# Local and selected attention of a head as one stream with one exponential over two score banks

## The reference, cut to what matters

```python
o_cmp, p_cmp = compressed_attention(q, k_cmp, v_cmp, slopes)      # 127 compressed keys
sel_idx = select_blocks(p_cmp, T)                                 # top 16 of 32 blocks of 64 keys
o_slc = selected_attention(q, k_slc, v_slc, sel_idx, slopes)      # softmax over the selected blocks
o_win = window_attention(q, k_win, v_win, slopes)                 # softmax over the last 512 keys
gates = sigmoid(g + gate_b)
o_nsa = gates[..., 0:1] * o_cmp + gates[..., 1:2] * o_slc + gates[..., 2:3] * o_win
```

## Time and profile before

| | |
|---|---|
| median of 3 runs | 1835.87 us (1835.27 to 1837.19) |
| the profiled execution's own time | 1841.42 us |
| its span, slowest core | 1840.4 us (cores 1823.4 to 1840.4) |
| PE busy | 1728.9 us, 94% |
| DVE busy | 684.4 us, 37% |
| ScalarE busy | 503.2 us, 27% |
| POOL busy | 141.4 us, 8% |
| exponentials of L926 | 272 |

### The profile page before, as it was taken

One profiled execution on the slowest core, in us unless ns is written; L12 is line 12 of the kernel. 1 busy time (PEld: TensorE's weight loads), 2 busy tenths in 40 slices (PEclk: granted clock), 3 DMA queues, 4 the chain that ended last, 5 costly groups with the idle time before them and its releaser, 6 DMA issues.

```text
span 1840.4 us, 27742 instructions; the slowest of 8 cores (1823.4 to 1840.4 us)
## 1 busy us (share of the span) xinstructions
PE 1728.9 (94%) x10082; PEld 885.7 (48%) x10082; DVE 684.4 (37%) x1257; ACT 503.2 (27%) x834; POOL 141.4 (8%) x157
## 2 busy tenths in 40 slices
PE   4999989999787888998899999999999999999999
PEld 1374746554665763443344444444444444444444
DVE  2333122011676767323535151433415151433415
ACT  4151244232787954446510000000000000000000
POOL 5101101000000010000000000001010000001000
PEclk9999999999999998999999999999999999999999
DMA  9954789754501189438360928557491928467464
GB/s 135 142 53 46 87 98 115 76 80 68 111 2 31 20 164 156 114 47 115 46 88 13 129 31 107 62 77 87 51 118 26 131 35 103 59 79 87 52 92 183
DMA packets 204852, 152.53 MB, mean 83 GB/s; under 512 B 14320, under 2 KB 188848, under 8 KB 204592
## 3 DMA queue, kind: packets, MB, share of 16 engines
q0 software_dynamic: 186320, 126.00, 55.3%
q1 hardware_dynamic: 18400, 24.75, 5.0%
HBM read 265.92 MB, written 8.45 MB: 149 GB/s over the span
## 4 chain that ended last, share of the span: by engine, by line
PE 86%; DMA 4%; DVE 3%; ACT 3%; issue 2%; POOL 1%; DVEq 0%; ACTq 0%; POOLq 0%
PE psum L1293 17%; PE psum L1275 17%; PE psum L1273 17%; PE psum L479 15%; PE psum L1114 6%; PE psum L486 3%; PE psum L923 3%; PE psum L819 3%; DMA arena<-xT 2%; PE psum L1188 2%; PE psum L1239 1%; DMA arena<-memT 1%; DMA arena<-cwx 1%; ACT arena L926 1%; PE psum L1075 1%
## 5 line engine op out<-in xcount | busy, mean ns | idle before, releaser
L1101 DVE TENSOR_TENSOR arena<-psum,arena 128x512 f32<-128x512 f32 x432 | 298.2, 691 | 137.1 <-PE psum L1114 64.7
L479 PE MATMUL psum<-arena 128*128 128x512 bf16 (+2 forms) x1600 | 312.9, 355 | 9.7 <-DVE arena L527 7.2
L1275 PE MATMUL psum<-arena 128*128 128x512 bf16 x1408 | 318.3, 379 | 0.0
L1273 PE MATMUL psum<-arena 128*128 128x512 bf16 x1408 | 318.2, 379 | 0.0
L1293 PE MATMUL psum<-arena 128*128 128x512 bf16 x1408 | 305.7, 379 | 0.0
L1280 ACT ACTIVATE arena<-psum 128x512 bf16<-128x512 f32 x88 | 52.6, 598 | 824.2 <-PE psum L1273 804.5
L1281 DVE TENSOR_TENSOR arena<-psum,arena 128x512 bf16<-128x512 f32 x88 | 60.8, 691 | 536.2 <-PE psum L1273 429.6
L479 PEld LDWEIGHTS psum<-arena 128*128 128x128 bf16 x1600 | 147.2, 99 | 167.2 <-issue 23.4
L1293 PEld LDWEIGHTS psum<-arena 128*128 128x128 bf16 x1408 | 137.8, 98 | 166.1
L1275 PEld LDWEIGHTS psum<-arena 128*128 128x128 bf16 x1408 | 137.7, 98 | 166.2
L1273 PEld LDWEIGHTS psum<-arena 128*128 128x128 bf16 x1408 | 137.8, 98 | 165.9
(11 more groups left out here) (142 smaller groups left out, 1102.9 us busy)
## 6 DMA issues: line engine op xcount, KB each, us to landing
arena<-w_gate POOLq DMA_DIRECT2D x22, 1024.0 KB, 20.0
arena<-w_up POOLq DMA_DIRECT2D x22, 1024.0 KB, 24.0
arena<-w_down POOLq DMA_DIRECT2D x22, 1024.0 KB, 14.5
arena<-w_in POOLq DMA_DIRECT2D x18, 1024.0 KB, 15.1
arena<-cwx POOLq DMA_DIRECT2D x10, 864.0 KB, 12.7
arena<-xT POOLq DMA_DIRECT2D x32, 256.0 KB, 40.4
arena<-xo SPq DMA_DIRECT2D x32, 256.0 KB, 7.6
arena<-w_out POOLq DMA_DIRECT2D x8, 1024.0 KB, 34.6
```

Of the source, the lines that this page charges most:

```text
L479: op(PE, lambda: nc.tensor.matmul(bank[psi][:, 0:n], lhsT=wt[:, kc, cc * 128:(cc + 1) * 128], rhs=rhs(kc), start=(kc == 0), stop=(kc == 15 ...
L1101: op(DVE, lambda: nc.vector.tensor_tensor(out=dst, in0=bank[psi][:, :], in1=dst, op=ALU.add), r=[bankb[psi]], w=[xrb[d][tc]])
L1273: op(PE, lambda: nc.tensor.matmul(bank[pg][:, :], lhsT=wgt[:, kc, cc * 128:(cc + 1) * 128], rhs=h3T[tc][kc // 4][:, kc % 4, :], start=(kc ...
L1275: op(PE, lambda: nc.tensor.matmul(bank[pu][:, :], lhsT=wut[:, kc, cc * 128:(cc + 1) * 128], rhs=h3T[tc][kc // 4][:, kc % 4, :], start=(kc ...
```

## The change

Window and selected branch of a head and half become one `stream`. Its jobs 0 to 4 hold both branches at one distance: scores in two neighbouring banks, selected first, one exponential over both into a `Pt` tile twice as wide, then selected and window products into two accumulator pairs, `s` and `w`, which change places at the start of each stream. The window branch is read out after job 4, the selected one after the last job. Scores (and transposes) rotate over banks 0 to 3. Iteration n now issues `pvf` of job n-3, there are six `Pt` tiles, and the due times of `later` are shorter.

The compressed job of half 0 comes after job 5 of its stream and uses the pair `w`. Of half 1, the compressed jobs of heads 0 and 1 open the stage, those of 2 and 3 come in the tail of head 0's first stream, and those of heads 4 to 7 (group 1) after job 8 of group 0's streams of half 1, so there are eight `oc1` tiles. The output `catA` takes the place of the queries `qnT`, and `M` is allocated after the convolution's input is freed.

```diff
-        qnT = self.tile(A, "qnT", [128, NH, TQ], BF16)
+        CT = self.scope()
+        qnT = self.tile(CT, "qnT", [128, NH, TQ], BF16, hi=True)
...
-        M = self.tile(AT, "selM", [128, 16, 512], BF16)
-        Mb = self.buf("selM")
...
-        NP_ = 8
-        Pt = [self.tile(AT, f"Pt{j}", [128, 512], BF16) for j in range(NP_)]
+        NP_ = 6
+        Pt = [self.tile(AT, f"Pt{j}", [128, 2, 512], BF16) for j in range(NP_)]
         Ptb = [self.buf(f"Pt{j}") for j in range(NP_)]
         rot_P = Rot(range(NP_))
-        rot_S = Rot([0, 1, 6])
-        rot_O = Rot([2, 4])
-        rot_T = Rot([7])
-        oc1 = [self.tile(AT, f"oc1_{j}", [128, 4, 128], F32) for j in range(4)]
-        oc1b = [self.buf(f"oc1_{j}") for j in range(4)]
+        sring = {"p": 0}
+        opair = {"s": 4, "w": 6}
+
+        def s_pair():
+            p = (sring["p"] + 1) // 2 * 2 % 4
+            sring["p"] = (p + 2) % 4
+            return p
+
+        def s_one():
+            p = sring["p"]
+            sring["p"] = (p + 1) % 4
+            return p
+
+        def o_swap():
+            opair["s"], opair["w"] = opair["w"], opair["s"]
+
+        oc1 = [self.tile(AT, f"oc1_{j}", [128, 4, 128], F32) for j in range(8)]
+        oc1b = [self.buf(f"oc1_{j}") for j in range(8)]
...
-        CT = self.scope()
-        catA = self.tile(CT, "catA", [128, 8, TQ], BF16, hi=True)
-        catTb = [[self.buf(f"catT{c}_{t}") for t in range(2)] for c in range(16)]
+        M = self.tile(AT, "selM", [128, 16, 512], BF16)
+        Mb = self.buf("selM")
+        catA = qnT
+        catTb = qnTb + [[self.buf(f"catT{c}_{t}") for t in range(2)] for c in range(8)]
         later = []
 
-        def run_jobs(jobs, L=5):
+        def run_jobs(jobs, L=3):
...
-                st["b0"] = rot_O.next()
-                si = rot_S.next()
+                si = s_one()
...
             def pvf(pj):
-                b0 = st["b0"]
-                pv(pj, 0, b0, lambda j: vcaug[:, g, 0:nv], lambda j: [vcaugb], nv, True, True)
-                rj = finish(b0, nv, h, tc, 0, oc, ocbuf, "first")
+                if swap:
+                    o_swap()
+                b0 = opair["w"]
+                pv(pj, 0, 0, b0, lambda j: vcaug[:, g, 0:nv], lambda j: [vcaugb], nv, True, True)
+                rj = finish(b0, nv, h, tc, 0, oc, ocbuf, "first" if tc == 1 else "add")
                 if tc == 1:
...
+        def stream(g, h, tc, oc, ocbuf, at=None):
+            for dl in range(qts[3] + 1):
                 j0 = min(j for j in range(4) if qts[j] >= dl)
+                last = dl == qts[3]
+                parts = [1, 0] if dl <= 4 else [1]
+
+                def sc(dl=dl, j0=j0, parts=parts):
+                    si = s_pair() if len(parts) == 2 else s_one()
+                    n0 = j0 * 128
+                    for part in parts:
+                        bi = si + (1 - part if len(parts) == 2 else 0)
+                        idx = g if part else 2 + g
+                        if dl == 0:
+                            op(PE, lambda: nc.tensor.matmul(bank[bi][:, :], lhsT=ident, rhs=TRI, start=True, stop=False, skip_group_check=True), r=[cbb, cidb], w=[bankb[bi]])
+                        for j in range(j0, 4):
+                            kt = qts[j] - dl
+                            op(PE, lambda: nc.tensor.matmul(bank[bi][:, j * 128:(j + 1) * 128], lhsT=KnT[:, idx, kt * 128:(kt + 1) * 128], rhs=qnT[:, h, tc * 512 + j * 128:tc * 512 + (j + 1) * 128], start=(j == j0 and dl > 0), stop=(j == 3), skip_group_check=True), r=[KnTb[idx][kt // 4], qnTb[h][tc]], w=[bankb[bi]])
                     pj = rot_P.next()
+                    ba = pvec[:, PV_AB + h * 16 + dl:PV_AB + h * 16 + dl + 1]
+                    if len(parts) == 2:
+                        src = psum[:, si * 512:(si + 2) * 512].rearrange("p (b n) -> p b n", b=2)[:, :, n0:512]
+                        op(ACT, lambda: nc.scalar.activation(out=Pt[pj][:, :, n0:512], in_=src, func=AF.Exp, bias=ba), r=[bankb[si], bankb[si + 1], pvb], w=[Ptb[pj]])
                     else:
+                        op(ACT, lambda: nc.scalar.activation(out=Pt[pj][:, 0, n0:512], in_=bank[si][:, n0:512], func=AF.Exp, bias=ba), r=[bankb[si], pvb], w=[Ptb[pj]])
+                    if tc == 1 and dl > 0:
                         md = mdiag(dl, j0)
+                        pvw = Pt[pj][:, 0, n0:512]
                         if md is not None:
                             p4 = pvw.rearrange("p (b j n) -> p b j n", j=2, n=128) if j0 == 0 else pvw.rearrange("p (j n) -> p j n", n=128)
                             op(DVE, lambda: nc.vector.tensor_tensor(out=p4, in0=p4, in1=md, op=ALU.mult), r=[Mb], w=[Ptb[pj]])
...
+                    if dl == 4:
+                        pvw = Pt[pj][:, 1, n0:512]
+                        op(DVE, lambda: nc.vector.tensor_tensor(out=pvw, in0=pvw, in1=WIN[:, n0:512], op=ALU.mult), r=[cbb], w=[Ptb[pj]])
                     return pj
 
+                def pvf(pj, dl=dl, j0=j0, parts=parts, last=last):
+                    if dl == 0:
+                        o_swap()
+                        st["s"], st["w"] = opair["s"], opair["w"]
+                    for part in parts:
+                        b0 = st["s" if part else "w"]
+                        vs = g if part else 2 + g
+                        pv(pj, 1 - part, j0, b0, lambda j: Vaug[:, qts[j] - dl, vs, :], lambda j: [Vaugb[qts[j] - dl]], NV, dl == 0, last if part else dl == 4)
+                    if dl == 4:
+                        finish(st["w"], NV, h, tc, 2, oc, ocbuf, "add" if tc == 1 else "first")
                     if last:
+                        cj = rot_ocb.next()
+                        finish(st["s"], NV, h, tc, 1, oc, ocbuf, "last", ocb[cj], ocbb[cj])
+
+                        def outT():
+                            tb2 = s_one()
...
+                        later.append([4, outT])
                 jobs.append((sc, pvf))
+                for f in (at or {}).get(dl, ()):
+                    f()
...
-                later.append([1 + 2 * j, lambda j=j: one(j)])
+                later.append([1 + j, lambda j=j: one(j)])
...
-            later.append([11, mbuild])
+            later.append([7, mbuild])
+        def c1(h, swap=False):
+            g = h // 4
+            cmp_job(g, h, 1, oc1[h], oc1b[h], post=(lambda: topk(g)) if h % 4 == 3 else None, swap=swap)
+
+        c1(0, True)
+        c1(1, True)
         for g in range(2):
-            c1 = lambda hl: cmp_job(g, 4 * g + hl, 1, oc1[hl], oc1b[hl], post=(lambda g=g: topk(g)) if hl == 3 else None)
-            c1(0)
             for hl in range(4):
                 h = 4 * g + hl
                 o_, ob_ = oc0[hl % 2], oc0b[hl % 2]
-                cmp_job(g, h, 0, o_, ob_)
-                branch_jobs(g, h, 0, 2, o_, ob_)
-                c1(1 if hl == 0 else 3) if hl < 2 else None
-                branch_jobs(g, h, 0, 1, o_, ob_)
-                c1(2) if hl == 0 else None
+                at = {5: [lambda: cmp_job(g, h, 0, o_, ob_)]}
+                if h == 0:
+                    at[6] = [lambda: c1(2)]
+                    at[7] = [lambda: c1(3)]
+                stream(g, h, 0, o_, ob_, at)
             for hl in range(4):
-                branch_jobs(g, 4 * g + hl, 1, 2, oc1[hl], oc1b[hl])
-            for hl in range(4):
-                branch_jobs(g, 4 * g + hl, 1, 1, oc1[hl], oc1b[hl])
+                h = 4 * g + hl
+                stream(g, h, 1, oc1[h], oc1b[h], {8: [lambda: c1(4 + hl)]} if g == 0 else None)
```

More of the change, by code:

```diff
@@ L813, in acc_view, with pv @@
             return psum[:, b0 * 512:(b0 + 2) * 512].rearrange("p (b n) -> p b n", b=2)[:, :, 0:2 * nv].rearrange("p b (j n) -> p b j n", j=2)
-        def pv(pj, j0, b0, vap, vbufs, nv, first, last):
+        def pv(pj, part, j0, b0, vap, vbufs, nv, first, last):
             for j in range(j0, 4):
@@ L818, in pv @@
                 o0 = (j % 2) * nv
-                op(PE, lambda: nc.tensor.matmul(bank[ob][:, o0:o0 + nv], lhsT=Pt[pj][:, j * 128:(j + 1) * 128], rhs=vap(j), start=(first and j % 2 == 0), stop=last, skip_group_check=True), r=[Ptb[pj]] + vbufs(j), w=[bankb[ob]])
+                op(PE, lambda: nc.tensor.matmul(bank[ob][:, o0:o0 + nv], lhsT=Pt[pj][:, part, j * 128:(j + 1) * 128], rhs=vap(j), start=(first and j % 2 == 0), stop=last, skip_group_check=True), r=[Ptb[pj]] + vbufs(j), w=[bankb[ob]])
         def finish(b0, nv, h, tc, br, oc, ocbuf, mode, dst=None, dstb=None):
@@ L881, in sc @@
                 pj = rot_P.next()
-                op(ACT, lambda: nc.scalar.activation(out=Pt[pj][:, :], in_=bank[si][:, :], func=AF.Exp), r=[bankb[si]], w=[Ptb[pj]])
+                op(ACT, lambda: nc.scalar.activation(out=Pt[pj][:, 0, :], in_=bank[si][:, :], func=AF.Exp), r=[bankb[si]], w=[Ptb[pj]])
                 return pj
             def pvf(pj):
-                b0 = st["b0"]
-                pv(pj, 0, b0, lambda j: vcaug[:, g, 0:nv], lambda j: [vcaugb], nv, True, True)
```

(10 more changed lines are left out.)

48 lines of the change are left out of this document (5 added, 43 removed).

## The result

| | before | after |
|---|---|---|
| median | 1835.57 us (1834.71 to 1837.19) | 1883.43 us (1881.41 to 1884.9) |
| the profiled execution's own time, its span | 1841.4, 1840.4 us | 1884.2, 1883.2 us |
| spans of the eight cores | 1823.4 to 1840.4 us | 1866.8 to 1883.2 us |
| exponentials of the streams | 272 | 192 |

The changed kernel is slower: the medians lie 47.9 us apart where 22.4 were forecast. The ratio of the two kernels is 1.0249, 95% interval 1.0234 to 1.0263, which is 45.7 us. The direction was right, the size was not, and the time lies above the range. Ratios leave out executions in which the cores of a die ran at a lower clock throughout; in keep_busy_tails two of six remain.

A forecast was written before the change was run, and what follows sets the result against it. No engine fills the 197.3 us attention stage; waits between engines bound it. Streams +20.4 (half 1) and +12.8 (half 0), compressed jobs -10.8 make +22.4: 1841.4 to 1863.8, less 5.5 to the median, 1858 us; range 1843 to 1873.

The forecast's parts named there:

- The waits: Half 1 stream: PE stands 2.1 us at the start, ScalarE dry 1.9, then dry 1.7 behind the window reading.
- The signs named in advance: 80 fewer exps, about 1.1 us a pair; accumulator-reading waits 16 to 25 us; ScalarE idle over 50 us.
- Faster: Rival: accumulators are read in time, leaving only ScalarE's saving of 12.8 us; 1823 us, chance 0.12.
- the clock, made a rival: Rival: PE's stands bring the lower clock, costing 1 us each, 16 times; 1874 us, chance 0.15.
- Half 0's other terms: Half 0: streams 8.6 us against 7.0 (+12.8 in all); start 3.3, jobs in head 0's tail 5, group 0's selection 1.
- The walk of a head: Half 1 stream followed step by step: 14.85 us a head against 12.3 before, +20.4 us in all.
- A pair's exponential: Exponential over two banks: 1.00 us where two cost 1.16, 80 times, at most 12.8 us of ScalarE.
- Stands kept by choice: Half 1: unexplained PE stands of 3.2 and 1.3 us, and some 0.9 lost at half clock, kept in the forecast.
- The compressed jobs: Moved compressed jobs and selections: 23.8 us against 34.6, -10.8; in masked tails 2.5 each, group 1's selection 4.5.
- costs two: Rival: an exponential over two banks costs as much as two, +7.7 us on the walked chain; 1866 us, chance 0.1.

The follow-up runs named there:

- keep_busy_tails: Kernel after with unread 512-column matmuls where PE stands at stream starts, before job 8's products, behind selections and in some tails; ratio 1.0220.
- late_window: Kernel after with the window products of job 0 issued one job later, after the selected products of job 1; ratio 1.0135.
- masks_last: Kernel after with each iteration's masks issued on DVE after its products and reading instead of before; ratio 1.0172.
- cmp_early: Kernel after with group 1's compressed jobs and selection in the tails of group 1's first two half 0 streams; ratio 1.0257.
- late_mirror: late_window with group 1's compressed jobs placed like group 0's, two before its first half 0 stream and two in its tail; ratio 1.0124.
- two_exps: Kernel after with one exponential per score bank instead of one over two banks; ratio 1.0261.
- before_split: Kernel before with both adds of each reading issued three iterations later; ratio 0.9960.
- mirror_split: mirror_masks_last with half 1's window reading put behind its iteration's mask and its add three iterations later; ratio 1.0076.
- mirror_masks_last: late_mirror with the masks issued after the products; ratio 1.0109.

## Why the prediction was right and wrong

- **The waits: right.** PE stands on L850 and behind the window's reading, once each in the head shown, at the places and within 0.3 us of the lengths walked; late_window and masks_last halve the first and give back 21 and 14 us. The signs named in advance came: 80 fewer exponentials, 1.115 us for a pair, 21.4 us on L850, ScalarE idle for 89 us. "Faster" rested on the accumulators being read in time; the waits on L850 and late_window show the opposite.
- **The step that failed: the clock, made a rival at 0.15 and 1 us a stand.** It was set against the forecast as another case, where it comes on top of every stand of the forecast. The argument against it, that the earlier trace rows has stands of 1.1 us in a stretch at 1.00, says nothing of stands twice as long, which the walk itself produced. Stands of 1.09 us were followed by it too, on core 5 and not on core 1. The stretches at clock 1.00 of keep_busy_tails put it at 10.5 us in half 1 on core 5, and the head shown on two cores adds 1.6 us in half 0: 12.1 us of clock shown, where the rival as priced would have had 16.
- **Half 0's other terms: mis-sized.** Its stretches on core 5 lie 3.7 and 5.2 us above the walk. By heads (ident matmul to ident matmul) the start is 1.4 us shorter than walked, head 0 takes its 13.6, and head 1 takes 14.2 where 9.6 were walked: in it PE stands 3.19 us behind a row of readings on DVE (compressed job 2, the selected branch, compressed job 3 with its L911), and the 6.7 us after have a clock of 0.55. Group 0's jobs and selection were priced at 6 us and cost 4.6 more. Group 1's first head takes 11.2 us (walked 8.6) at 0.61, the third the 1.6 us of clock named; plain heads at 1.00 take 8.8 to 9.2, so the walk of 8.6 was near. How the two heads at 0.76 and 0.61 divide into clock and waits stays open, as no core shows them at 1.00.
- **The walk of a head, too short by little.** At clock 1.00 a head takes 15.6 us (core 2 after) against 14.85. In keep_busy_tails, at 1.00, the last stretch is 66.95 us against 63.5 forecast, or 62.2 without the stand of 1.3 us: 4.75 us. The second is 75.8 against 78.0, or 73.9 without the stands of 3.2 and 0.9. A pair's exponential has a mean of 1.115 us and follows the next after some 1.03, three percent above 1.00.
- **Stands kept by choice: wrong.** 5.4 us of unexplained stands and lower clock were carried over and did not recur; the other cores of the kernel before didn't have the stands either. So the sum on core 5 is: forecast 22.4, less 5.4, plus 10.5 (clock, half 1), 8.9 (half 0) and 6.6 (walk of half 1) make 43.0, the stage's growth. The other 5 us to 47.9 come from the base: the profiled execution of before was 5.9 us above the median of 1835.57 (5.5 above the one that the prediction had), that of after 0.8. The change was sized against one profile, and taking its distance to the median as a constant cost that much.
- **The compressed jobs: roughly right where they are, not looked at from the other side.** They were priced at 2.5 us each in masked tails, with 4.5 for the selection; cmp_early's heads of group 0 are 14.6 us shorter than after's for 14.5 priced (core 4 against core 5). late_mirror's 1.0124 against late_window's 1.0135 says that the other places cost about as much.
- **The exponential: the rival "costs two" was priced at 7.7 us, and two_exps shows 2 by the ratio and 5 by the stage.** It was priced on the chain as ScalarE's pace; that PE's waits end last and hide part of it is argued, not shown.

Left open: which stands of PE are followed by the lower level. That the loss would be gone with a third accumulator pair wasn't tried: the eight banks are all in use.

## What to carry to other kernels

Before two branches are merged to save instructions, ask what their buffers did between them: a pair that rotates hides a reading, and a pair that is refilled at once shows it. On an engine that works its queue in order, issue what frees a bank ahead of what nobody waits for, and put the second half of a reading later; that paid off in the old kernel (before_split) and in the new one (mirror_split). Every stand of PE that a walk produces should be followed by the question of what clock comes after it, and that cost belongs in the forecast, not beside it.

## What the runs showed of the hardware that was not expected

- In the kernel after the clock fell in the 3.5 us behind a stand of PE of 1.86 us (1.00 to 0.56). In masks_last it stayed at 1.00 through a head with stands of 1.36 and 1.74 us and one with 0.86 and 1.66 us. In masks_last two stands of 2.31 us were seen as well: what followed the first (537 to 554 us) stayed at 1.00. In the kernel after, a stand of 1.09 us was followed by a fall on core 5 and by none on core 1. So the length alone doesn't decide; that the fall comes with stands far shorter than the 3.2 and 4.5 us of the earlier trace rows was the surprise.
- Unread matmuls held the clock at 1.00 and were worth 10 us in the kernel after, and cost 7 us in mirror_masks_last, where the clock of half 1 was at 0.98 and 1.00 without them.
- An add of 128x512 f32 took 1.36 us on POOL against 0.69 on DVE, and DVE's masks 552 ns against 420 while POOL worked beside them.
